# Hybrid decoder step on one core: key roots by a power on GpSimd, and the first attention one unit later

## The reference

```python
z = rmsnorm(x, g_mix_norm) @ w_in                     # uv, q, three k/v pairs, gates
u, v = gelu(uv) halves; v = rmsnorm(v, g_sgu)
o_a = u * (tril(w_sgu) @ v per chunk of 128 + b_sgu)  # gated MLP
ks = rmsnorm(kvs[:, :, 0], g_k[1]); kw = rmsnorm(full_w[:, :, 0], g_k[2])
# attention: compressed, selected and window branch, 8 heads, T5 bias, gates per head
o_b = g0 * softmax(q kc + b) vc + g1 * softmax(q ks + b) vs + g2 * softmax(q kw + b) vw
x = x + (sigmoid(g_a) * (o_a @ w_proj_gmlp) + sigmoid(g_b) * (o_b @ w_proj_nsa)) @ w_out
y = x + square(relu(rmsnorm(x, g_mlp_norm) @ w_up)) @ w_down
```

## Time and profile before

| | us |
|---|---|
| median of 3 runs | 2619.91 (2619.55 to 2620.23) |
| the profiled execution's own time | 2619.55 |
| its span, first to last instruction | 2618.1 |
| TensorE busy | 2597.4 |
| VectorE busy | 1954.0 |
| ScalarE busy | 1404.1 |
| GpSimd busy | 465.2 |

### The profile page before, as it was taken

The page is one execution under the profiler, slowest core; times in us unless marked ns, Lnnn a source line. Parts: engine busy times, 40 slices in busy tenths (PEclk is TensorE's granted clock), DMA queues, the critical chain, the costliest instruction groups (busy, mean ns, idle before and its releaser), DMA issues. The chain is left out here.

```text
span 2618.1 us, 57445 instructions
## 1 busy us (share of the span) xinstructions
PE 2597.4 (99%) x21488; PEld 2569.3 (98%) x21488; DVE 1954.0 (75%) x2894; ACT 1404.1 (54%) x2414; POOL 465.2 (18%) x632
## 2 busy tenths in 40 slices
PE   9999999999999999999999999999999999999998
PEld 9999989999999999999999999999999999999998
DVE  6455645667877764446588888888898888888888
ACT  6435435555545442222266666566666666666656
POOL 2001360001111210023301121121211212212113
PEclk9999999999999999999999999999999999999999
DMA  6533452113333444434435665765756657567568
GB/s 220 192 112 108 154 179 77 61 58 131 116 123 123 144 156 143 137 123 142 135 103 142 166 164 146 177 148 161 174 141 171 158 147 179 147 167 171 140 167 181
DMA packets 125309, 378.73 MB, mean 145 GB/s; under 512 B 14258, under 2 KB 15922, under 8 KB 124928
## 3 DMA queue, kind: packets, MB, share of 16 engines
q1 hardware_dynamic: 69328, 245.36, 27.8%
q0 software_dynamic: 52688, 126.18, 22.5%
q10 hardware_dynamic: 3168, 5.45, 0.6%
HBM read 292.22 MB, written 91.00 MB: 146 GB/s over the span
## 5 line engine op out<-in xcount | busy, mean ns | idle before, releaser
L2731 DVE TENSOR_TENSOR w_lo<-w_raw,w_hi 128x1024 fp32r<-128x1024 f32 x351 | 429.2, 1225 | 105.6 <-ACT w_hi L1876 104.3
L1876 ACT ACTIVATE w_hi<-w_raw 128x1024 fp32r<-128x1024 f32 x352 | 370.8, 1062 | 203.2 <-PE aux L1353 72.1
L2051 DVE TENSOR_TENSOR w_lo<-w_raw,w_hi 128x512 fp32r<-128x512 f32 x280 | 201.9, 724 | 341.1 <-ACT w_hi L1498 340.2
L1353 PE MATMUL aux<-at_t,w_hi 128*128 128x260 f32 x2304 | 416.6, 282 | 0.1
L1498 ACT ACTIVATE w_hi<-w_raw 128x512 fp32r<-128x512 f32 x280 | 175.3, 628 | 420.6 <-PE mm L938 400.2
L938 PE MATMUL mm<-a_hi,w_hi 128*128 128x260 f32 x1728 | 358.0, 288 | 0.0
L1353 PEld LDWEIGHTS aux<-at_t,w_hi 128*128 128x128 f32 x2304 | 355.0, 188 | 0.4 <-DVE w_lo L2731 0.3
L1417 PE MATMUL aux<-fb_mid,w_hi 128*128 128x260 f32 x1920 | 352.1, 283 | 1.4 <-DVE w_lo L2731 1.1
L938 PE MATMUL mm<-a_hi,w_lo 128*128 128x260 f32 x1728 | 348.4, 283 | 0.0
L938 PE MATMUL mm<-a_lo,w_hi 128*128 128x260 f32 x1728 | 347.8, 283 | 0.0
L1353 PE MATMUL aux<-at_t,w_lo 128*128 128x260 f32 x1152 | 325.4, 282 | 0.0
(11 more groups left out here) (482 smaller groups left out, 5852.2 us busy)
## 6 DMA issues: line engine op xcount, KB each, us to landing
w_raw<-in_w_ff SPq DMA_DIRECT2D x256, 512.0 KB, 3.5
w_raw<-in_w SPq DMA_DIRECT2D x142, 512.0 KB, 3.5
out_y_t<-y_mid POOLq DMA_DIRECT2D x120, 520.0 KB, 8.0
w_raw<-in_w_st SPq DMA_DIRECT2D x56, 512.0 KB, 4.3
g_in<-merge_d POOLq DMA_DIRECT2D x16, 520.0 KB, 4.7
merge_d<-z POOLq DMA_DIRECT2D x18, 260.0 KB, 3.8
st_f<-in_x_p POOLq DMA_DIRECT2D x8, 520.0 KB, 4.7
pages<-in_cache_cmp POOLq DMA_DIRECT2D x16, 256.0 KB, 4.2
```

Source lines behind the costliest of these rows:

```text
L1353: last = pe.matmul(dst, w, at_t[:, j, e:e + HT], start=FRESH[b] and j == 0 and part == 0, stop=j == KP - 1 and part == 2, skip_group_check ...
L1876: run(hi_of(p, k), source(p, k), ACT.Copy).then_inc(ff_hi, 1)
L2051: dve.tensor_tensor(w_lo[:, c, :], raw(u, c), w_hi[:, c, :].bitcast(F32), ALU.subtract).then_inc(lo_split, 1)
L2731: dve.tensor_tensor(lo_of(p, k), source(p, k), hi_of(p, k).bitcast(F32), ALU.subtract).then_inc(ff_lo, 1)
```

## The change

1. The first guess of the key roots is made by GpSimd, as `k_a` to the power -0.5 against a column of -0.5 (`smp_roots`), behind the last key load and ahead of the last `load_flat`. ScalarE's `smp_guess_roots` goes.
2. `smp_key_roots` goes from the first chunk of host unit 4 to the last of unit 3. TensorE's `smp_turn_roots` goes from the hook behind the third chunk of unit 4 to the one behind its first, ahead of that chunk's scores; `smp_roots_in` likewise.
3. `smp_exps` goes behind the gelu of unit 4 and the first split of the next; `smp_divide` one split later.
4. The attends start one hook earlier and come one to a hook; `smp_pick`, `smp_copy`, `smp_result`, `first_head` and the last norm each move to a later hook.
5. Attention step 0 moves out of unit 8: `scores(0)` stands at the head of unit 9, its softmax and exponentials at k-step 0, `v_norm` at 1 and `divide` at 4. `turn_probs(0)` stays at 7.
6. On GpSimd `load_values(6)` comes before `v_squares(5)`; the memset of `p_c` moves from unit 7 to the end of unit 8.

```diff
@@ TensorE
             for i in range(1, DEC // 2 + 1):
-                dense(i, [lambda: smp_scores(2 * i - 2), smp_bias if i == 2 else None,
-                          lambda: (smp_turn_roots() if i == DEC // 2 else None, smp_scores(2 * i - 1))])
-            dense(5, [None, None, smp_turn_probs])
-            dense(6, [lambda: (smp_attend(0), smp_attend(1)), lambda: (smp_attend(2), smp_attend(3)),
-                      lambda: smp_attend(4), lambda: smp_attend(5)])
-            dense(7, [lambda: smp_attend(6), lambda: smp_attend(7), smp_pick])
+                dense(i, [lambda: (smp_turn_roots() if i == DEC // 2 else None, smp_scores(2 * i - 2)),
+                          smp_bias if i == 2 else None, lambda: smp_scores(2 * i - 1)])
+            dense(5, [None, None, smp_turn_probs, lambda: smp_attend(0)])
+            dense(6, [lambda: smp_attend(1), lambda: smp_attend(2), lambda: smp_attend(3), lambda: smp_attend(4)])
+            dense(7, [lambda: smp_attend(5), lambda: smp_attend(6), lambda: smp_attend(7)])
...
+            dense(DEC, [smp_pick, None, last_norm])
...
-            dense(DEC, [None, last_norm, lambda: scores(0)])
...
-                if r == 0 and a:
+                if r == 0:
                     scores(a)
...
-                dense(N_SMP + n,
+                dense(N_SMP + n, first_hook=None if n else (lambda: between(0)),
                       among=lambda c, k: between(KT * n + CK * c + k + 1))
@@ ScalarE
-            def smp_guess_roots():
-                act.wait_ge(smp_base, 1)
-                steps.did(run(k_r[:, :], k_a[:, :], ACT.Ln))
-                run(k_r[:, :], k_r[:, :], ACT.Exp, scale=-0.5).then_inc(smp_guess, 1)
...
+            act_jobs = {2: [None, smp_bias_in], 4: [smp_roots_in], 5: [smp_exps]}
...
-            act_jobs = {2: [None, smp_bias_in], 3: [None, None, smp_guess_roots],
-                        4: [None, None, smp_roots_in, smp_exps], 7: [first_head]}
...
+            beside(host(DEC), [None, first_head, lambda: guess(N_NORM_V)])
...
-            beside(host(DEC), [None, lambda: guess(N_NORM_V), lambda: exps(0, 0)])
...
-                if r == 0 and a:
+                if r == 0:
                     exps(a, w)
@@ VectorE
-                                 lambda: (smp_norms(2 * i + 1), smp_mean() if last else None)],
-                       first=lambda: smp_norms(2 * i))
+                                 lambda: (smp_norms(2 * i + 1), smp_mean() if last else None), None,
+                                 smp_key_roots if last else None], first=lambda: smp_norms(2 * i))
...
-            beside(host(4), [smp_key_roots, None, None, smp_softmax])
+            beside(host(4), [None, None, None, smp_softmax])
...
-            beside(host(5), [smp_divide, None, smp_probs_out])
+            beside(host(5), [None, smp_divide, smp_probs_out])
...
-            beside(host(7), [None, smp_copy, lambda: (steps.did(dve.memset(p_c[:, :, :], 0.0)), smp_result())])
+            beside(host(7), [None, None, None, smp_copy])
             tile_out(7)
+            beside(host(DEC), [smp_result, None, lambda: mean(N_NORM_V, D_GM)])
+            tile_out(DEC)
+            steps.did(dve.memset(p_c[:, :, :], 0.0))
...
-            beside(host(DEC), [None, lambda: mean(N_NORM_V, D_GM), lambda: softmax(0, 0, 0), v_norm])
-            tile_out(DEC)
...
-                if r == 0 and a:
+                if r == 0:
                     softmax(h, a, w)
-                if r == (4 if a else 0):
+                if r == 1 and a == 0:
+                    v_norm()
+                if r == 4:
@@ GpSimd
+            steps.did(pool.memset(minus_half, -0.5))
...
+            def smp_roots():
+                pool.wait_ge(smp_base, 1)
+                pool.tensor_tensor(k_r[:, :], k_a[:, :], minus_half[:, 0:1].to_broadcast([P, NPG * 2 * NKV * DEC]), ALU.pow
+                                   ).then_inc(smp_guess, 1)
...
             load_keys(DEC - 1)
+            smp_roots()
             load_flat(DEC - 1)
...
+            load_values(6)
             v_squares(5)
-            load_values(6)
```

More of the change, by code:

```diff
@@ L343, in build @@
         rl = small[:, 12:15]
+        minus_half = small[:, 56:64]
         w00 = small[:, 64:72]
@@ L1667, in _ @@
             tile_out(0)
+            act_jobs = {2: [None, smp_bias_in], 4: [smp_roots_in], 5: [smp_exps]}
+            for i in range(1, DEC):
+                beside(host(i), act_jobs.get(i, ()))
+                tile_out(i)
             def first_head():
@@ L1672, in first_head @@
                 copy_queries(0)
-            act_jobs = {2: [None, smp_bias_in], 3: [None, None, smp_guess_roots],
-                        4: [None, None, smp_roots_in, smp_exps], 7: [first_head]}
-            for i in range(1, DEC):
-                beside(host(i), act_jobs.get(i, ()))
-                tile_out(i)
+            beside(host(DEC), [None, first_head, lambda: guess(N_NORM_V)])
+            act.wait_ge(smp_read, 2)
+            tile_out(DEC)
             def exps(a, w):
@@ L1685, in exps @@
                 last.then_inc(s_exp, 1)
-            beside(host(DEC), [None, lambda: guess(N_NORM_V), lambda: exps(0, 0)])
-            act.wait_ge(smp_read, 2)
-            tile_out(DEC)
             def probs_out(a, w):
```

## The result

The kernel after takes 2633.15 us (median of 5 runs, 2631.14 to 2634.69); the kernel before, beside it, 2619.55 us (5 runs, 2617.70 to 2620.23). The ratio is 1.0053, 95% interval 1.0039 to 1.0068: 13.6 us slower, and above the range that was given (2632). The profiled execution took 2632.53 us against 2619.55, its span 2630.8 against 2618.1.

What follows compares the result with a forecast made beforehand. TensorE, busy 2597.4 of 2618.1 us, was taken as the bound, so only its waits and low clock count. The terms +0.45 + 0.7 + 1.0 = +2.15 gave 2621.7, as a median 2622.1 us; range 2617.5 to 2632.

Steps and rivals of the forecast that it cites:

- P: Length of GpSimd's power for the key roots: taken as 2.1 us, between 0.43 and 9.7.
- a hundred plain steps: Upper end for GpSimd's power at the key roots: each element passes through that many plain steps, 9.7 us.
- the power is long: Rival at the key roots: each microsecond of P is one of stall; 2629.7 us at 9.7; chance 0.26.
- P - 0.25: Stall in us at the roots' transposes if power and `w_lo` don't exclude each other; the larger of 0.95 and this.
- 0.95 + P: Stall in us at the roots' transposes if power and `w_lo` shut each other out; taken, 3.05 against 2.6.
- the power and `w_lo` don't exclude each other: Rival at the key roots: stall 1.85 us, total 2620.9 us; chance 0.08.
- Part 2: Samples' softmax behind host unit 4: wait of about 1.1 us at the samples' probabilities against 0.4, +0.7 us.
- Part 3: First attention, opening host unit 9: stall 3.3 us at `turn_probs(0)` against 2.3, +1.0 us.
- D: End of host unit 8, from which the first attention's times were counted.
- D + 1.7: ScalarE through with the last norm's guess 1.7 us after unit 8 ends, delaying unit 9's last weight split.
- The low clock: TensorE at half clock behind the waits at roots and `turn_probs(0)`: kept as before, 0; high at samples' probabilities.
- The rest: Attends spread over hooks, value loads, `first_head`, `smp_pick`, `smp_result`, `v_squares(7)`: inputs in time, no matmul added or removed, 0.

Runs made afterwards that it cites:

- e5: Kernel after with GpSimd's power cut into three instructions of 16, 16 and 32 columns: 2632.59 us, run once.
- e4: Kernel after with a product in place of GpSimd's power, same shape and place, so the key roots are not computed: 2622.08 us.
- e10: e9 with GpSimd's squares of v for chunks 0 and 1 moved behind load_values(3): 2616.08 us.
- e12: e9 with seven of the eight v_squares calls later still, two between the loads of the last values and five behind them: 2611.67 us.
- e13: Kernel after with the last norm one chunk earlier, behind the second chunk of unit 8, where the kernel before has it: 2631.09 us.
- e2: Kernel before with only ScalarE's guess of the roots replaced by GpSimd's power, everything else in its old place: 2626.71 us.
- e7: Kernel before with smp_key_roots called right behind the last tile of unit 3: 2618.43 us.
- e9: Kernel before with smp_key_roots right behind unit 3's last tile, and v_norm, divide(0) and the copy of the values moved earlier: 2616.34 us.
- e11: Kernel before with the move of attention step 0 alone; key roots, power and key row sums as before: 2620.78 us.

## Why the prediction was wrong

**The step that failed** is the size of the power: "I take some 19 steps, P = 2.1 us, nearer the plain row". It took 10.95 us, five times that, and above the 9.7 us that were to be the upper bound. The plain row priced a plain operation; nothing in the trace priced a power. Measured by e5, the power's slope is 0.157 us a column where the plain operation's is 1.46 ns, some 107 times. The upper bound, worked out from "a hundred plain steps", was the better guess, though no row gave the hundred either, so that it came within 1.3 us is luck; the forecast took a value near the other end with no row for it. The rival "the power is long" was the right one, at 0.26. Its 2629.7 for P = 9.7 is 3.4 us short. That its wait of 0.95 + 9.7 = 10.65 us nearly meets the measured 10.75 is chance: the P was 1.25 us too short and the form, as the next paragraph shows, 1.2 us too long.

**Right in mechanism and place.** The wait is one microsecond for each of P, to 3%: from e4's product to the power the instruction grew by 10.3 us (0.66 to 10.95) and the wait by 9.95 (0.8 to 10.75). Of the two forms given for it the one without exclusion held: P - 0.25 makes 10.7 us and the trace has 10.75; 0.95 + P would have made 11.9. The mean was done at 341.16, forecast 341.0. So the rival "the power and `w_lo` don't exclude each other" (0.08) was right about that, and only with a wrong P. The Trainium skill says that a VectorE instruction with two inputs in SBUF and a GpSimd one that reads SBUF exclude each other (SBUF — State Buffer, "Who interferes with whom"). For the power this case's rows decide against it, 1.38 us for two `w_lo` that started at 341.08, the second wholly inside the power, with 0.69 us each as elsewhere. For GpSimd's sums of squares e10's first row, above, agrees with it: the two-input instruction took 1.05 us where e12's took 0.16. The other two long rows have one input in SBUF, and that sentence does not speak of them. Why the power differs, no run shows.

**Part 2** was right in size: a wait of 1.38 us, forecast 1.1 (+1.0 over before in place of +0.7). The chain ran as worked out: 9.3 us from the start of the first `w_lo` behind unit 4 (366.34) to the end of the divide (375.60), where the prediction has 9.4 with the squares. The squares account for about 1.0 us of the wait, by an estimate from rows: the softmax's long instruction took 1.04 us (0.46 in e12) and the `w_lo` ahead of the divide 1.08 (0.69 elsewhere), both beside them. No run has the order of the kernel after with the squares out of the way.

**Part 3** was short by 1.0 us: wait 4.3, forecast 3.3. The softmax did start at D + 3.8 (425.38), as worked out. But the gelu's table load was left out of ScalarE's chain. It waits for `z`, so gelu and second load end at D + 6.9 and not at D + 5.45: 1.45 us later. TensorE resumed at D + 12.1 and not at D + 10.9, 1.2 us later, and since it came to the wait 0.2 us later too (D + 7.8), the wait shows 1.0. The trace of before had that load too, at 419.84, behind a wait of 3.55 us for `z`; the chain in the prediction took the table as already loaded. In the kernel before:

```profile
419.84 1.28 ACT L1644 ACT_TABLE_LOAD   x1 [3.55 <-DVE z L2078]
```

The move of the norm, which the prediction did carry as its "D + 1.7", is 1.4 us of the 4.3 (e13).

**The low clock** was forecast unchanged. TensorE worked at it for 5.3 us behind the last wait and 3.7 behind the first, in place of 3.1 and 3.4: +1.2 us. No run shows what made it longer.

**The rest, forecast as 0.** The loads stayed hidden, as said: nothing of the kernel after waits for `load_flat(7)`. In e2, without TensorE's own lateness, it does, for 3.3 us. Some 0.5 us over the sum of waits and clock is left unexplained; that it comes from the attends spread over more hooks was not tested.

With P = 10.95 and the form without exclusion the prediction's own sum would have been 8.1 + 0.7 + 1.0 = 9.8 us, 2629.7. Measured is 3.4 us more by the medians and 2.9 by the spans of the two profiled executions. The latter is, to 0.1 us, 1.0 at part 3, 1.2 of clock, 0.3 at part 2 and the 0.5.

## What to carry to other kernels

An operation that the trace has never shown is not priced by its nearest plain neighbour: if it lies on the chain that the fast engine waits for, give the far bound the larger share, or time it alone first. Where a wait is won, look at what TensorE reaches next and whether the engine that feeds it is held there, as e10 gave back at the samples' divide all that it won at the roots. When a job is called one unit later, redo the chain with the table loads in it, and ask for each whether it stands behind a wait.

## What was not expected of the hardware

- GpSimd's power costs 0.157 us a column of 128 partitions, against 0.66 us for the whole product of 64 columns.
- VectorE's two-input `w_lo` ran at full speed during the power, while a one-input operation (0.27 us alone) took 1.35 us beside GpSimd's two-input sum.
- The clock does not follow the length of a wait alone. Behind the 1.7 us wait of e7 it was 0.61, behind the 1.7 us wait of e9 it stayed at 1.00; behind the 2.9 us of e11 it was 0.74, behind the 2.9 us of e13 1.00, where it had been 0.51 behind a wait of 1.6 us shortly before. Each is one execution of its kernel, and the clock differs between executions of one kernel as well: over e9's eleven its mean over the whole run was 0.998 to 1.000. So one trace does not price the clock behind a wait. Windows of e7 and of e9 behind the same wait:

```profile
352.00:355.00 3.00, 3.00 (x22) 2.80 (x15) 1.02 (x2) 0.12 (x1) 2.02 (x4) 0.61 0.42 108
```

```profile
350.00:354.00 4.00, 3.70 (x33) 3.13 (x34) 2.05 (x4) 0.38 (x1) 2.15 (x5) 1.00 0.30 81
```
